# Queries and keys of the second block by seven block products, with each slab's rotation behind the next slab's products

## The reference, cut to what matters

```python
def attention_mixer(h, hc, w_qkv, w_o, sinks, cos, sin, with_ctx_out):
    q, k, v = jnp.split(h @ w_qkv, [Q_DIM, Q_DIM + N_KV_HEADS * HEAD_DIM], axis=-1)
    q = axial_rope(q.reshape(b, L, N_HEADS, HEAD_DIM), cos, sin)
    k = axial_rope(k.reshape(b, L, N_KV_HEADS, HEAD_DIM), cos, sin)
    ...
    kc, vc = jnp.split(hc @ w_qkv[:, Q_DIM:], 2, axis=-1)
    ...
    qc = (hc @ w_qkv[:, :Q_DIM]).reshape(b, C, N_KV_HEADS, Q_PER_KV, HEAD_DIM)
```

## Time and profile before

| | us |
|---|---|
| median of 3 runs | 2844.55 |
| lowest to highest | 2843.97 to 2847.08 |
| the profiled execution | 2842.85 |
| span of its trace | 2840.7 |
| PE busy | 2668.2 (94%) |
| DVE busy | 1421.2 (50%) |
| ACT busy | 511.5 (18%) |

### The profile page before, as it was taken

One profiled execution on the slowest core, in us unless ns is written; L12 is line 12 of the kernel. 1 busy time (PEld: TensorE's weight loads), 2 busy tenths in 40 slices (PEclk: granted clock), 3 DMA queues, 4 the chain that ended last, 5 costly groups with the idle time before them and its releaser, 6 DMA issues. The chain is left out here.

```text
span 2840.7 us, 37338 instructions
## 1 busy us (share of the span) xinstructions
PE 2668.2 (94%) x15588; PEld 1980.1 (70%) x15588; DVE 1421.2 (50%) x2811; ACT 511.5 (18%) x1175; POOL 247.0 (9%) x292
## 2 busy tenths in 40 slices
PE   5999999899898999989988899999999899999998
PEld 4778886684487888758544554688888466665983
DVE  1355443876524734466340472555533358873751
ACT  1251210010013321101002351200000333421000
POOL 1001110120000112011000000000000025420000
PEclk9999999899998999989999999999999999999999
DMA  5322114677542210358771101122222253433542
GB/s 205 110 89 90 47 32 137 217 241 249 192 126 89 90 61 17 116 185 263 239 248 50 40 1 45 60 90 89 82 82 83 71 161 120 123 101 127 176 157 96
DMA packets 276959, 340.65 MB, mean 120 GB/s; under 512 B 7189, under 2 KB 227349, under 8 KB 276665
## 3 DMA queue, kind: packets, MB, share of 16 engines
q1 hardware_dynamic: 264880, 309.61, 33.9%
q10 hardware_dynamic: 8760, 17.64, 1.9%
q0 software_dynamic: 3152, 11.01, 1.1%
HBM read 337.05 MB, written 1.19 MB: 119 GB/s over the span
## 5 line engine op out<-in xcount | busy, mean ns | idle before, releaser
L403 PE MATMUL PS<-MEM 128*128 128x512 f32 x1072 | 463.7, 593 | 8.9 <-POOL MEM L2437 2.8
L374 PE MATMUL PS<-MEM 128*128 128x256 f32 x1760 | 399.7, 389 | 9.2 <-DMA MEM<-w_up 7.5
L1159 ACT ACTIVATE MEM<-PS 128x256 f32<-128x256 f32 (+4 forms) x421 | 177.6, 437 | 1258.9 <-PE PS L374 266.2
L403 PEld LDWEIGHTS PS<-MEM 128*128 128x128 f32 x1072 | 202.6, 190 | 265.4 <-issue 250.5
L374 PEld LDWEIGHTS PS<-MEM 128*128 128x128 f32 x1760 | 342.2, 196 | 63.0 <-DMA MEM<-w_up 11.2
L896 PE MATMUL PS<-MEM 128*128 128x256 f32 (+1 forms) x2352 | 386.1, 327 | 0.0
L896 PEld LDWEIGHTS PS<-MEM 128*128 128x128 f32 x2352 | 353.7, 190 | 32.7 <-issue 0.5
L1647 DVE SCALAR_TENSOR_TENSOR MEM<-MEM 128x256 f32<-128x256 f32 x560 | 265.2, 507 | 12.0
L875 PE MATMUL PS<-MEM 128*128 128x512 f32 (+2 forms) x496 | 182.4, 527 | 4.6 <-ACT MEM L1364 4.6
L580 PE MATMUL PS<-MEM 128*128 128x256 f32 x768 | 172.3, 382 | 0.0
L1056 PE MATMUL PS<-MEM 128*128 128x512 f32 (+1 forms) x512 | 171.0, 486 | 0.0
(11 more groups left out here) (339 smaller groups left out, 2884.9 us busy)
## 6 DMA issues: line engine op xcount, KB each, us to landing
MEM<-w_in SPq DMA_DIRECT2D x54, 1024.0 KB, 5.4
MEM<-ada_w SPq DMA_DIRECT2D x48, 1024.0 KB, 5.3
MEM<-w_up SPq DMA_DIRECT2D x32, 1024.0 KB, 7.1
MEM<-w_down SPq DMA_DIRECT2D x32, 1024.0 KB, 5.2
MEM<-ssm_w_in SPq DMA_DIRECT2D x24, 1024.0 KB, 5.4
MEM<-ffn_gate SPq DMA_DIRECT2D x22, 1024.0 KB, 5.3
MEM<-ffn_up SPq DMA_DIRECT2D x22, 1024.0 KB, 5.2
MEM<-ffn_down SPq DMA_DIRECT2D x20, 1024.0 KB, 5.1
```

The source lines that it names most:

```text
L374: ins = pe.matmul(bank[:, 0:T], W[:, k, c * P:(c + 1) * P], XT[:, k, :], start=k == 0, stop=k == KT - 1)
L403: ins = pe.matmul(banks[t], src(kk, t), W[:, k, :], start=kk == 0, stop=kk == nk - 1)
L1159: act.activation(out, view(b), func, **kw).then_inc(S("bank_read_by_act"), 1)
```

## The change

- The key slab and the four query slabs go through `seven_products` in place of `channels2`. `SEVENS`, the list of all such slabs, gets five entries of kind "qk" in the order keys (s = 4), then queries 0 to 3. Their semaphore counts stand ahead of those of the feed-forward, and for that the parity of the buffers of `DSUM`, which lie over `WSUM`, is flipped.
- The value slab is the first of the six, where it was the last.
- `rotated(s)` issues the two `ROT` products of slab s. It stands behind the products of the slab after it, and for the last slab behind the rotation of the one before. DVE's `roped(s)` stands behind the joining of the next slab in the same way.
- DVE's joining of a slab is a function `joined`, which the feed-forward calls too. After each "qk" slab DVE raises `qk_joined`, for which `rotated` waits.
- ACT no longer copies queries and keys out of PSUM. It copies the first product of each slab, three of them ahead of the doubling of the keys and two behind it.

```diff
-        SEVENS = [(l, kind, s) for l in range(2) for s in range(NF2 // 2) for kind in ("fg", "fu") if s or kind == "fu"]
+        SEVENS = [(0, "qk", s) for s in (4, 0, 1, 2, 3)] + [(l, kind, s) for l in range(2) for s in range(NF2 // 2) for kind in ("fg", "fu") if s or kind == "fu"]
...
-                if (kind, s) == ("fu", 0):
-                    pe.wait_ge(S("x_summed"), l + 1)
+                if n in (QK7[0], FFN7[0][0], FFN7[1][0]):
+                    pe.wait_ge(S("x_summed"), 1 + (n > QK7[-1]) + l)
...
             gate_rows(0, 0, 2, 2)
             turn_normed(0, 2)
-            for s in range(4):
-                channels2(io["w_qkv"], 256 * s, 256, [("q2", 2 * s), ("q2", 2 * s + 1)], ("act",) * 2)
-            channels2(io["w_qkv"], QD, 256, [("k2", 0), ("k2", 1)], ("act",) * 2)
             W = a_slab(io["w_qkv"], QD + 256)
             for t in range(4):
...
-            pe.wait_ge(S("const2_loaded"), 80)
-            for c in range(2):
-                emptied(pe, ("k2", c))
-                bank = take(("rk", c), "dve")
-                done(pe.matmul(bank[:, 0:T], ROT, KF[:, c, 0:T], start=True, stop=True))
-            for c in range(8):
-                emptied(pe, ("q2", c))
-                bank = take(("rq", c), "dve")
-                done(pe.matmul(bank[:, 0:T], ROT, QF[:, c, 0:T], start=True, stop=True))
+            def rotated(s):
+
+                pe.wait_ge(S("const2_loaded"), 80)
+                pe.wait_ge(S("qk_joined"), (s + 1) % 5 + 1)
+                for c in range(2 * s, 2 * s + 2):
+                    src = KF[:, c - 8, 0:T] if c >= 8 else QF[:, c, 0:T]
+                    bank = take(("rot", c), "dve")
+                    done(pe.matmul(bank[:, 0:T], ROT, src, start=True, stop=True))
+
+            for i in QK7:
+                seven_products(io["w_qkv"], 256 * SEVENS[i][2], 0, "qk", SEVENS[i][2])
+                if i > QK7[0]:
+                    rotated(SEVENS[i - 1][2])
+            rotated(3)
...
-            for c in range(8):
-                copy(("q2", c), QF[:, c, :])
-            for c in range(2):
-                copy(("k2", c), KF[:, c, :])
             for t in range(4):
                 copy(("v2", t), VV[:, t, :], lambda b: b[:, 0:T])
+            for i in QK7[:3]:
+                p1(i)
             act.wait_ge(S("k_roped"), 2)
...
+            for i in QK7[3:]:
+                p1(i)
...
-            for c in range(2):
-                roped(c, ("rk", c), ("k2", c), KF[:, c, 0:T], c, "k_roped")
-            for c in range(8):
-                roped(c, ("rq", c), ("q2", c), QF[:, c, 0:T], c, "q_roped")
+            for i in QK7:
+                c = 2 * SEVENS[i][2]
+                o = KF if c == 8 else QF[:, c:c + 2, :]
+                joined(i, [o[:, j // 2, T * (j % 2):T * (j % 2) + T] for j in range(4)], (lambda: weights(i + 1)) if i < QK7[-1] else (lambda: None))
+                dve.nop().then_inc(S("qk_joined"), 1)
+                if i > QK7[0]:
+                    dve.wait_ge(S("const2_loaded"), 80)
+                    roped(SEVENS[i - 1][2])
+            roped(3)
```

More of the change, by code:

```diff
@@ L329, in build, with sevens_of @@
         seven_at = []
-        SEVENS = [(l, kind, s) for l in range(2) for s in range(NF2 // 2) for kind in ("fg", "fu") if s or kind == "fu"]
+        SEVENS = [(0, "qk", s) for s in (4, 0, 1, 2, 3)] + [(l, kind, s) for l in range(2) for s in range(NF2 // 2) for kind in ("fg", "fu") if s or kind == "fu"]
+        def sevens_of(l, kinds):
+            return [i for i, e in enumerate(SEVENS) if e[0] == l and e[1] in kinds]
+        QK7, FFN7 = sevens_of(0, ("qk",)), [sevens_of(l, ("fg", "fu")) for l in range(2)]
         w_in, w_branch, w_out, w_up, w_down = io["w_in"], io["w_branch"], io["w_out"], io["w_up"], io["w_down"]
@@ L1375, in feed_forward_sevens @@
                     copy(("fg", l, f), HID2[:, f, 0:2 * tn], lambda b: b[:, 0:2 * tn], ACT.Silu)
[L1376 to L1380 removed]
+                p1(FFN7[l][0])
+                for i in FFN7[l]:
                     _, kind, s = SEVENS[i]
[L1382 to L1389 removed]
+                    if i < FFN7[l][-1]:
                         p1(i + 1)
@@ L2058, in feed_forward_sevens, with weights @@
-                first = l * len(SEVENS) // 2
-                mine = range(first, first + len(SEVENS) // 2)
-                weights(first)
-                for i in mine:
+            def weights(i):
+                at = seven_at[i]
+                dve.wait_ge(S(f"slab_loaded{at % NSLOT}"), 16 * (at // NSLOT + 1))
+                W = RING[:, at % NSLOT, :].rearrange("p (k n) -> p k n", k=KT)
+                a11, a21, a12, a22 = [W[:, k:k + 4, c:c + P] for k in (0, 4) for c in (0, P)]
+                q = lambda j: WSUM[:, i % 2, j, :, :]
+                dve.tensor_tensor(q(2), a11, a21, ALU.subtract)
+                link(dve.tensor_tensor(q(0), a21, a22, ALU.add))
+                link(dve.tensor_tensor(q(1), q(0), a11, ALU.subtract))
+                dve.tensor_tensor(q(3), a12, q(1), ALU.subtract).then_inc(S("w_summed"), 1)
@@ L2062, in feed_forward_sevens @@
+            def feed_forward_sevens(l):
+                n = 2 * l + 1
+                tn = P if l else T
+                rms(n, NT * (2 - l), 2 - l)
+                modulated(n, 2 - l)
+                emptied(dve, ("nT", n, 1 - l, 2))
+                x_sums(tn)
+                weights(FFN7[l][0])
+                for i in FFN7[l]:
                     _, kind, s = SEVENS[i]
@@ L2181, in _, with roped @@
             modulated(0, 2)
[L2182 to L2196 removed]
+            emptied(dve, ("nT", 0, 1, 2))
+            x_sums(T)
+            weights(0)
+            def roped(s):
+                for c in range(2 * s, 2 * s + 2):
+                    x = KF[:, c - 8, 0:T] if c >= 8 else QF[:, c, 0:T]
+                    b = filled(dve, "dve", ("rot", c))
+                    read(dve.tensor_tensor(RT[:, c % 2, :], b[:, 0:T], SIN, ALU.mult))
+                    link(dve.tensor_tensor(x, x, COS, ALU.mult))
+                    settle()
+                    dve.tensor_tensor(x, x, RT[:, c % 2, :], ALU.add).then_inc(S("k_roped" if c >= 8 else "q_roped"), 1)
+            for i in QK7:
[7 more added lines that the diff above has]
+            roped(3)
             def maxes2(h):
```

111 lines of the change are left out of this document (43 added, 68 removed).

## The result

| | us |
|---|---|
| before, median of 4 runs | 2844.26 (2840.90 to 2847.08) |
| after, median of 4 runs | 2826.99 (2824.55 to 2832.86) |
| ratio after to before, with its 95% interval | 0.9943 (0.9924 to 0.9962) |
| the profiled execution after, and its span | 2832.86, 2830.8 |

The kernel is 0.57% faster, 17.3 us between these medians; the interval runs from 10.8 to 21.6 us. Executions of one kernel differ by several us, so the two traces, one execution of each kernel, need not differ as the medians do: their spans are 9.9 us apart, 2840.7 and

A forecast was written before the change was run, and what follows sets the result against it. PE, busy 94% of the span, bounds the kernel, but DVE's ropes set the attention loop's start. PE's 5.72 us (8.30 − 2.58) plus the tail's 6.75 make 12.47; 2844.55 − 12.47 = 2832.1 us, range 2828.5 to 2837.5.

The forecast's parts named there:

- the sum: Query/key/value stage up to head 0's maxima: gain 12.47 us, 5.72 from PE and 6.75 behind the last slab.
- The steps costed at nothing: In the projections, DVE's sums, interleaved ropes, ACT's copies and weight loads were to cost PE 0 us.
- the 8.6 us of the prediction: In each slab, DVE's ropes could last until about 8.6 us after the previous slab before PE waits.
- The whole rest should move by that amount: From head 0's maxima on, the unchanged program was to run 12.47 us earlier, giving a span of 2828.2.
- the last of the sum: Whole kernel: the earlier median of 2844.55 less the 12.47 us gain gives 2832.1 us.
- The allowance of 3.5 us either way: Attention loop: PE's low-clock periods might shift, one 3 us longer or shorter changing the time by 1.5 us.
- The tail did shrink: Rival, behind the last slab: something other than DVE's ropes starts the loop, only −5.7 us, 2838.8; chance 0.06.
- PE did not wait: Rival, in the five slabs: PE waits 1.5 to 2.5 us each for DVE, result 2840 to 2845; chance 0.05.
- The clock did not fall in the projections: Rival, in the five slabs: short waits bring PE to 1.2 GHz, 2892.7 if all five; chance 0.03.
- The rule of the Trainium skill: Projections: by that page PE's brief idling swings the clock, so the 0.03 slower rival would be the forecast.
- The gap ahead of the first turned probabilities: Start of the attention loop: one PE wait of 5.6 us was to replace those of 3.89 and 3.12.

The follow-up runs named there:

- The two parts, taken alone: Against the kernel before: only the seven products, ropes and rotations all behind the last slab, ratio 0.9964; only the new order with eight products, ratio 0.9989.
- e_slack10: Changed kernel with 10 additional unused DVE multiplications behind each of the first three rope pairs; stage 82.40 us, one run of 2834.64 us.
- e_slack20: Changed kernel with 20 additional unused DVE multiplications behind each of the first three rope pairs; stage 99.99 us, one run of 2842.67 us.
- e_values_last: Changed kernel with the value products behind the last rotation instead of in front; stage 88.88 us, median 2835.96 us, 0.9981 of before.
- v_split: Changed kernel with half the value products behind head 1's logits and the last rope pair behind head 0's maxima; median 2819.97 us, 0.9928 of before.
- v_values: Changed kernel with only the value products cut in two, half moved behind the logits of head 1; median 2822.45 us, 0.9930 of before.
- same_after: Changed kernel run again without any edit; stage 82.40 us, median 2828.64 us over 5 runs, 0.9953 of before.
- v_rope: Changed kernel with only the last rope pair moved behind head 0's maxima and its rotation products behind head 0's logits; median 2829.07 us, 0.9951 of before.

## Why the prediction was wrong

- **The direction and the mechanism held.** Every step of the sum up to the gain has its counterpart in the trace. A slab by seven products takes 12.11 us, the values 13.89, the last slab ends 77.05 us after the first product (76.97 in the sum), the maxima follow after 5.35 (5.26), the stage is 82.40 (82.23). The two parts, taken alone, gave 8.14 and 4.21 us and add up.
- **The steps costed at nothing cost nothing.** DVE's sums ended 6.3 us early. The join with two ropes left DVE waiting 1.28 us for PE, and e_slack10 and e_slack20 put the point at which PE waits between 4.6 and 9.2 us of further work, by the length of the waits at 5.6; the 8.6 us of the prediction, less 3.0 for what is there, had put it at 5.6 too.
- **"The whole rest should move by that amount" held to about 3 us, not to the hundredth.** The rest was 1241.65 and 1241.63 us in the first pair of traces, 1242.40 and 1239.96 in the second, and 1239.01 to 1242.66 over all thirteen; the changed kernel alone has 1241.63 and 1239.96. Whether the 0.9 us between the 12.3 of the stage and the 13.2 of the larger sets is scatter is not shown.
- **The step that failed is the last of the sum**: 2844.55 − 12.47. It took the median of three runs as the kernel's time. Over 66 runs the kernel before has 2841.77, and single runs spread over 12.9 us, 2835.05 to 2847.95. From 2841.77 the same subtraction gives 2829.3, and the nine runs of after have 2828.57. The first four of them happened to have 2826.99, and so 17.3 us stand between medians of four runs each and 13.2 between the larger sets. With 2841.77 as its start, the same sum with the same allowance of 3.5 us would have reached down to 2825.8 and held the measured median.
- **The allowance of 3.5 us either way was mis-sized** for the same reason. It counted one period of low clock, where the traces show several things that move: the start of the stage by up to 9.8 us, the clock at the head of the loop, and again at the last head but one. The three runs that were shown spread over only 3.1 us, which told too little of a spread of 12.9. Two medians of a few runs each, the one that the forecast started from and the one that it was held against, were 2.8 and 1.6 us off the larger sets, in opposite directions. That they fell apart and not together was bad luck; that the forecast had no room for it was not.
- **The rivals.** The tail did shrink and PE did not wait, so the first two fell with the trace of after. The clock did not fall in the projections, where PE shows no gap: it was 1.00 from 1506 to 1590. e_slack20 and e_values_last show it falling in the same routine once PE waits 3.6 us or more, so this rival hung on the waits, and the slack kept them away. Its sum was off by a factor of two: if five slabs at half clock cost 60.6 us, one costs 12.1, so one slab would have taken the whole gain and not two. The rule of the Trainium skill on a clock that swings when PE idles briefly between groups of products ("TensorE: Matmul & The Clock Gate", "A second HAM failure mode: psum-queue depth-cycling") did not come true here for waits that were met before PE came to them. With the waits of 3.6 us of e_slack20 the clock did swing between 0.50 and 1.00; the page gives no length for its brief idling, so no run here shows whether that is the case it describes.
- **The gap ahead of the first turned probabilities** was forecast at 5.6 us and is 6.22, mostly because the logits of two heads were done 6.5 us after the last product of the slabs, not 7.0.

## What to carry to other kernels

Before trading PE time for additions on another engine, write down when within a period PE needs each sum and when that engine is free. The difference is the slack, and work up to it is free, as ten additional multiplications a slab showed. Work that the chain does not need yet, the values here, serves as a cover: half ahead of the first sums, half in the gap behind the logits. It did not surely keep the clock up there: it stayed at 1.00 in v_split's trace and fell in v_values'. And before a difference between two traces is put down to an edit, the same program should be traced twice: here a low clock of some 3 us at the last head but one came and went by itself and moved the loop by 1.64 us. Last, a forecast of less than half a percent needs the spread of single runs before it needs a better sum: three runs can lie 3 us off.

## What was not expected of the hardware

- A wait of 3.6 us on PE in dense work cost 5.9 us: 10.7 us of waiting made the stage 17.6 us longer (e_slack20), with the granted clock at 0.50 behind each wait (the three slabs were 5.6, 6.6 and 5.4 us longer). A wait of 5.63 us made the following work some 3 us longer (e_values_last).
- Much shorter waits were followed by a low clock too: 1.44 and 0.91 us of idling, with 2.8 us of logits between, by a clock of 0.50 from 1593.2 to 1596.3 in v_values. And the same wait of 2.98 us at the last head but one was followed by a low clock in nine traces and not in the other four; after and same_after, one program, are on different sides.
- A shorter gap did not spare the clock. Ahead of L1014 in v_rope PE idled 2.84 us, and the clock was 0.50 from 1593 to 1605. After 6.22 us of idling in the changed kernel it was back sooner in one execution than in the other. Busy time and clock of 1595 to 1602 and 1602 to 1612, in after and then in same_after:

```profile
1595.00:1602.00 7.00, 5.47 (x18) 3.86 (x19) 4.18 (x12) 2.76 (x10) 0.00 (x0) 0.62 0.00 0
1602.00:1612.00 10.00, 9.12 (x43) 5.47 (x42) 7.63 (x22) 5.24 (x15) 0.00 (x0) 1.00 0.01 2
```

```profile
1595.00:1602.00 7.00, 7.00 (x17) 3.93 (x15) 4.15 (x12) 4.00 (x12) 0.00 (x0) 0.50 0.00 0
1602.00:1612.00 10.00, 10.00 (x36) 5.73 (x36) 6.39 (x17) 4.12 (x12) 0.00 (x0) 0.77 0.01 2
```

- The same code reached the same point anywhere between 1498.6 and 1508.4 us. Waiting for weight loads may be one part of it, the rest is open.
